# A token mixer on 272 tokens in a row instead of three blocks of 128 with empty rows, attention heads in pairs, and a decay broadcast in one pass

## The reference, cut to what matters

```python
h = concat([meta, x])                                  # (272, 1024)
z, xbc, dt_raw, q_a, kv_a, gates = split(rms_norm(h) @ w_in)
xs, bm, cm = split(silu(causal_conv4(xbc)))            # 2048, 4*128, 4*128 channels
dt = softplus(dt_raw + dt_bias); a_cs = cumsum(-exp(a_log) * dt)
y[l] = sum(s <= l) (cm[l] . bm[s]) * exp(a_cs[l] - a_cs[s]) * dt[s] * xs[s]   # per head
y_ssd = group_norm((y + d_skip * xs) * silu(z)) @ w_ssd_out
q = rms_norm(q_a) @ w_uq;  k, v = rms_norm(c_kv) @ w_ukv   # 16 heads, 64 + 32 rope; k_pe shared
y_mla = softmax(causal(q @ k.T)) @ v @ w_o
h = h + (g_ssd * y_ssd + g_mla * y_mla) @ w_out
h = h + moe(rms_norm(h))                               # 32 experts, w1 8 MB and w2 4 MB each
out = rms_norm(h)[16:]
```

## Time and profile before

| | |
|---|---|
| median of 3 runs | 1399.79 us (1399.71 to 1402.7) |
| the profiled execution: its time, its span | 1400.83 us, 1399.0 us |
| busy in the span | PE 96%, VectorE 35%, ScalarE 23%, GpSimd 5% |
| granted PE clock, mean | 0.997 |
| HBM traffic | 461.8 MB moved, 330 GB/s on average, 416 to 419 GB/s from 490 us to the last 35 us |

### The profile page before, as it was taken

One profiled execution on the slowest core, in us unless ns is written; L12 is line 12 of the kernel. 1 busy time (PEld: TensorE's weight loads), 2 busy tenths in 40 slices (PEclk: granted clock), 3 DMA queues, 4 the chain that ended last, 5 costly groups with the idle time before them and its releaser, 6 DMA issues.

```text
span 1399.0 us, 18726 instructions
## 1 busy us (share of the span) xinstructions
PE 1337.8 (96%) x7131; PEld 652.9 (47%) x7131; DVE 484.5 (35%) x1217; ACT 320.9 (23%) x630; POOL 74.5 (5%) x88
## 2 busy tenths in 40 slices
PE   8999999999999999999999999999999999999995
PEld 5867778889994333333323222223222223333331
DVE  6847779998743212111211111111111211121112
ACT  4445547765321111111111011011001011011101
POOL 1000002322303000000000000000000000000000
PEclk9999999999999999999999999999999999999999
DMA  6332131334778899999999999999999999999995
GB/s 244 129 128 114 61 121 61 122 121 181 277 299 328 353 418 418 418 416 416 418 419 418 419 417 416 418 418 418 419 417 416 417 416 417 418 419 419 417 416 229
DMA packets 77410, 461.80 MB, mean 330 GB/s; under 512 B 6848, under 2 KB 6848, under 8 KB 41136
## 3 DMA queue, kind: packets, MB, share of 16 engines
q1 hardware_dynamic: 76608, 458.64, 80.8%
q0 software_dynamic: 752, 2.49, 0.5%
HBM read 460.05 MB, written 1.05 MB: 330 GB/s over the span
## 4 chain that ended last, share of the span: by engine, by line
PE 60%; DMA 19%; SPq 16%; DVE 2%; issue 2%; ACT 1%; ACTq 0%; DVEq 0%
PE bank L1299 57%; DMA ring<-w_dram 19%; SPq L405 9%; SPq L372 6%; PE bank L1614 1%; PE bank L1620 1%; PE bank L1425 1%; DMA work<-x_dram 0%; PE bank L1407 0%; PE bank L1636 0%; DVE split L887 0%; PE bank L1482 0%; DVE work L924 0%; PE bank L1326 0%; ACT split L553 0%
## 5 line engine op out<-in xcount | busy, mean ns | idle before, releaser
L1299 PE MATMUL bank<-ring,work 128*64 128x512 f32 (+3 forms) x2264 | 548.5, 591 | 34.5 <-DMA ring<-w_dram 32.1
L1299 PE MATMUL bank<-work 128*64 128x512 f32 (+7 forms) x2168 | 445.7, 558 | 6.2 <-issue 1.9
L1299 PEld LDWEIGHTS bank<-ring,work 128*64 128x64 f32 (+1 forms) x2264 | 176.7, 142 | 355.9 <-issue 259.7
L1299 PEld LDWEIGHTS bank<-work 128*64 128x64 f32 (+4 forms) x2168 | 151.3, 144 | 261.7 <-issue 245.6
L1247 DVE COPY work<-bank 128x256 f32<-128x256 f32 x32 | 13.6, 424 | 496.4 <-PE bank L1636 496.4
L1299 PE MATMUL bank<-hn_hi,split 128*128 128x256 f32 (+1 forms) x896 | 173.3, 289 | 0.9 <-DVE split L887 0.5
L1299 PEld LDWEIGHTS bank<-hn_hi,split 128*128 128x128 f32 x896 | 142.3, 190 | 1.7 <-issue 0.9
L1299 PE MATMUL bank<-hn_lo,split 128*128 128x256 f32 (+1 forms) x448 | 127.5, 285 | 0.0
L1221 DVE TENSOR_SCALAR work<-bank 128x256 f32<-128x256 f32 x64 | 24.2, 419 | 273.9 <-PE bank L1299 273.9
L887 DVE TENSOR_TENSOR split<-ring,split 128x1024 fp32r<-128x1024 f32 x80 | 99.1, 1240 | 26.0 <-ACT split L553 25.7
L739 ACT ACTIVATE work<-bank 128x512 f32<-128x512 f32 x32 | 19.1, 597 | 331.5 <-PE bank L1299 331.5
(11 more groups left out here) (250 smaller groups left out, 948.2 us busy)
## 6 DMA issues: line engine op xcount, KB each, us to landing
ring<-w_dram SPq DMA_DIRECT2D x256, 1024.0 KB, 21.4
work<-w_dram SPq DMA_DIRECT2D x128, 1024.0 KB, 19.9
ring<-slabs_dram SPq DMA_DIRECT2D x23, 2048.0 KB, 7.4
ring<-slabs_dram SPq DMA_DIRECT2D x2, 1152.0 KB, 5.2
ring<-slabs_dram SPq DMA_DIRECT2D x1, 1536.0 KB, 11.6
ring<-slabs_dram SPq DMA_DIRECT2D x1, 1280.0 KB, 8.4
work<-x_dram SPq DMA_DIRECT2D x2, 512.0 KB, 4.8
work<-x_dram POOLq DMA_DIRECT2D x2, 512.0 KB, 17.0
```

What stands on the lines that cost most here:

```text
L1299: return pe.matmul(o, lhsT, rhs, start=start, stop=stop)
```

## The change

- **Tokens in a row.** The sequence is 272 rows in blocks of 128, 128 and 16 (`BLOCKS`). Every matrix that had 384 columns or a third block of 128 rows has 272 or 16. The block order is (0, 1, 2). The queries start at row 16, so the products over earlier tokens are cut at 112 and 240: CB, `decay` and ssdy take 256, 144 and 16 columns. Empty rows are no longer set to zero. The factors for the queries (`rsxq`) come from two small matmuls with a shifted identity.
- **Heads in pairs.** `k_pair` makes the keys of two heads in one 128-wide matmul pair; the rope rows are laid out so that the odd head lies in the other half, and a query block is 128 rows. `pv_pair` runs for two heads with alternating halves of the output. The probabilities' transposes are three of 128 columns and two of 32 rows.
- **One-pass decay broadcast.** `AT` is made four times over (one per 32 partitions), high in two quarters and low in the other two, so that one matmul with 64 rows adds both parts.
- **One convolution tap on ScalarE.** `conv_in` makes the first tap and the bias with a second activation; `conv` has three buffers.
- Inputs' order: the first block of x and the meta tokens are loaded first.

```diff
-T = NB * P
-T0 = P - NMETA
+BLOCKS = [(0, P), (P, P), (2 * P, L - 2 * P)]
+TAIL = L - 2 * P
...
-        ORDER = (1, 2, 0)
+        ORDER = (0, 1, 2)
...
-            sp.dma_start(xtok[:, 1, :], x[0:P, :]).then_inc(x_in[1], 16)
+            sp.dma_start(xtok[NMETA:P, 0, :], x[0:P - NMETA, :]).then_inc(x_in[0], 16)
+            sp.dma_start(xtok[0:NMETA, 0, :], meta).then_inc(x_in[0], 16)
             sp.dma_start(vec[:, :], vecs).then_inc(vec_in, 16)
-            sp.dma_start(xtok[:, 2, :], x[P:2 * P, :]).then_inc(x_in[2], 16)
-            sp.wait_ge(meta_zero, 1)
-            sp.dma_start(xtok[T0:P, 0, :], meta).then_inc(x_in[0], 16)
+            sp.dma_start(xtok[:, 1, :], x[P - NMETA:2 * P - NMETA, :]).then_inc(x_in[1], 16)
+            sp.dma_start(xtok[0:TAIL, 2, :], x[2 * P - NMETA:SEQ, :]).then_inc(x_in[2], 16)
...
-                a.activation(xraw[:, c % 2, 3:3 + L], ps[:, 0:L], ACT.Copy).then_inc(proj_read, 1)
+                a.activation(xraw[:, c % 2, 3:3 + L], ps[:, 0:L], ACT.Copy)
...
+                if c >= 3:
+                    a.wait_ge(conv_fin, c - 2)
+                a.activation(conv[:, c % 3, :], ps[:, 0:L], ACT.Identity, scale=v("conv_w", 4 * c + 3, 1),
+                             bias=v("conv_b", c, 1)).then_inc(proj_read, 1)
...
-                a.activation(pT[:, 0:512], bank[4][:, :], ACT.Copy).then_inc(pTa_ready, 1)
+                a.activation(pT[:, h % 2, 0:3 * P], bank[4][:, 0:3 * P], ACT.Copy).then_inc(pTa_ready, 1)
...
-                link(d.tensor_scalar(dst, src[:, 3:3 + L], v("conv_w", 4 * c + 3, 1), v("conv_b", c, 1), ALU.mult, ALU.add))
...
-                d.tensor_copy(pT[:, 512:640], bank[5][:, 0:P]).then_inc(pTb_ready, 1)
+                d.tensor_copy(pT[0:TAIL, h % 2, 3 * P:PT_COLS], bank[5][0:TAIL, 0:64]).then_inc(pTb_ready, 1)
...
-                                CBm[:, c // CHUNKS_PER_GROUP, :].unsqueeze(1).to_broadcast([P, 2, 640]),
+                                CBm[:, c // CHUNKS_PER_GROUP, :].unsqueeze(1).to_broadcast([P, 2, DECAY]),
...
-            mm(bank[2][0:HEADS_S, 0:SEQ], dAb[0], metarows[:, :], True, False)
-            mm(bank[2][0:HEADS_S, P:SEQ], dAb[2], tri[:, 0:P], False, False)
-            mm(bank[2][0:HEADS_S, 0:SEQ], dAb[1], tri[:, :], False, True)
...
+            for i in range(4):
+                o = bank[2][i * HEADS_S:(i + 1) * HEADS_S, :]
+                mm(o[:, 0:SEQ], dAb[0], tri[:, NMETA:L], True, False)
+                mm(o[:, P - NMETA:SEQ], dAb[1], tri[:, 0:P + NMETA], False, False)
+                mm(o[:, SEQ - TAIL:SEQ], dAb[2][0:TAIL, :], tri[0:TAIL, 0:TAIL], False, True)
...
-                for k in range(KKV):
-                    mm(bank[6][0:NOPE, 0:L], ukv[:, k, h * NOPE:(h + 1) * NOPE], ckvT[:, k, T0:T], k == 0, k == KKV - 1)
+                for k in range(KKV):
+                    last = mm(bank[6][:, 0:L], ukv[:, k, i * P:(i + 1) * P], ckvT[:, k, :], k == 0, k == KKV - 1)
...
-                mm(o, vh[0], pT[:, 0:SEQ], True, False)
-                mm(o[:, P:SEQ], vh[2], pT[:, 2 * SEQ:2 * SEQ + P], False, False)
-                mm(o, vh[1], pT[:, SEQ:2 * SEQ], False, True).then_inc(pv_done, 1)
...
+                for b, rows, lo, at, cols in ((0, P, 0, 0, SEQ), (1, P, P, 2 * P, P), (1, TAIL, P - 32, 3 * P, 32),
+                                              (2, TAIL, SEQ - 32, 3 * P + 32, 32)):
+                    for j in range(2):
+                        last = mm(bank[3][j * VH:(j + 1) * VH, lo:lo + cols], V[0:rows, b, (2 * i + j) * VH:(2 * i + j + 1) * VH],
+                                  pT[0:rows, j, at:at + cols], at == 0, b == 2)
...
-                    row = head_row[:, 2 * c + j:2 * c + j + 1].to_broadcast([P, P])
-                    mm(bank[2 + 2 * j][:, 0:SEQ], row, AT_hi[:, :], True, False)
-                    last = mm(bank[2 + 2 * j][:, 0:SEQ], row, AT_lo[:, :], False, True)
+                    half = slice(j * 2 * E, (j + 1) * 2 * E)
+                    last = mm(bank[2 + 2 * j][:, 0:SEQ], head_row[half, 2 * c + j:2 * c + j + 1].to_broadcast([2 * E, P]),
+                              AT_hi[half, :])
```

More of the change, by code:

```diff
@@ L130, in meta_ssd_mla_moe @@
         ident2 = sb("ident2", E + 1)
-        small = sb("small", 804)
+        small = sb("small", 808)
         idx = sb("idx", 16, U32)
@@ L246, in meta_ssd_mla_moe @@
         nrt = sm(801, 3)
+        rsxq = sm(804, 2)
         def sem(name):
@@ L598, in _ @@
             a.wait_ge(latent_trans, 1)
-            for i in range(2):
-                a.activation(kTh[NOPE:QH, i, :], bank[7][NOPE:QH, T0:T], ACT.Copy).then_inc(kpeT_ready, 1)
+            a.activation(kTh[NOPE:P, 0, :], bank[7][NOPE:P, 0:L], ACT.Copy).then_inc(kpeT_ready, 1)
+            a.activation(kTh[0:NOPE, 1, :], bank[7][0:NOPE, 0:L], ACT.Copy).then_inc(kpeT_ready, 1)
             for c in range(4, 8):
@@ L613, in _ @@
             a.wait_ge(cum_read, 1)
-            a.activation(head_row[:, :], ident[:, 0:HEADS_S], ACT.Copy)
             a.activation(AT_hi[:, :], AT[:, :], ACT.Copy).then_inc(AT_hi_ready, 1)
@@ L838, in rstd_col @@
             def rstd_col(y, src, n, eps, done):
-                tmp = nrt[:, 0:1]
+                tmp = nrt[0:y.shape[0], 0:1]
                 yi = y.bitcast(I32)
@@ L1338, in _ @@
                     pe.wait_ge(rsx_ready, 3)
-                    for c in range(NB):
-                        last = mm(bank[6][:, c * P:(c + 1) * P], rsx[:, c:c + 1].to_broadcast([P, P]), ident[:, :])
-                    last.then_inc(rsx_spread, 1)
+                    for c, (s0, m) in enumerate(BLOCKS):
+                        mm(bank[6][:, s0:s0 + m], rsx[0:m, c:c + 1].to_broadcast([m, P]), ident[0:m, 0:m])
+                    mm(bank[7][:, 0:2], shifted[:, P:2 * P], rsx[:, 0:2], True, False)
+                    mm(bank[7][:, 0:2], shifted[0:NMETA, 0:P], rsx[0:NMETA, 1:3], False, True).then_inc(rsx_spread, 1)
             wsl = take("qa").rearrange("p (k n) -> p k n", k=KD)
@@ L1445, in _ @@
             for h in range(MH):
+                if h % 2 and h + 1 < MH:
+                    k_pair((h + 1) // 2)
                 if h + 1 < MH:
-                    qk_head(h + 1)
-                feature_unit("cv", 8 + h, 8 + h, T0)
-                if h:
-                    pv_head(h - 1)
+                    q_head(h + 1)
+                feature_unit("cv", 8 + h, 8 + h, 0)
+                if h and h % 2 == 0:
+                    pv_pair(h // 2 - 1)
                 if h + 1 < MH:
@@ L1453, in _ @@
                 probs_trans(h)
[L1454 to L1455 removed]
+            feature_unit("z", 0, PZ, NMETA)
+            pv_pair(KD - 1)
             pe.wait_ge(pv_read, KD)
             for g in range(GROUPS):
[L1460 to L1465 removed]
+                ps = bank[4 + g]
+                for (t0, n), (lo, at) in zip(BLOCKS, DECAY_AT):
+                    last = mm(ps[0:n, at:at + SEQ - lo], BT[:, g, t0:t0 + n], CT[:, g, lo:SEQ])
+                last.then_inc(cb_done, 1)
             def acum_of(c):
@@ L1480, in xtr_of @@
                     pe.wait_ge(xdt_ready, c)
-                for b in range(NB):
-                    last = pe.transpose(bank[6][:, b * P:(b + 1) * P], xT[:, c, b * P:(b + 1) * P], ident[:, :])
+                for b, (t0, n) in enumerate(BLOCKS):
+                    last = pe.transpose(bank[6][0:n, b * P:(b + 1) * P], xT[:, c, t0:t0 + n], ident[:, :])
                 last.then_inc(xtr_done, 1)
```

337 lines of the change are left out of this document (174 added, 163 removed).

## The result

The changed kernel took 1381.7 us (median of 4 runs, 1380.49 to 1382.79) beside 1401.24 us for the kernel before (1399.71 to 1403.13): the ratio is 0.9863, with a 95% interval of 0.985 to 0.9876. That is 19.5 us less where 24.5 were forecast; the time lies inside the range of 1363 to 1385 and 6.7 us above the 1375 predicted. Of these 6.7 us, 1.45 lie in the kernel before, whose median of four runs is 1401.24 where three had given 1399.79. Three disturbed executions (1470.72 us of experiment 11, and 4699.71 and 6317.84 us of the kernel before, measured again beside the experiments) are left out of the ratios. The profiled execution took 1382.37 us with a span of 1380.6, 18.4 us less than the span in the earlier trace rows.

A forecast was written before the change was run, and what follows sets the result against it. The PE was taken to set the mixer and weight loads the experts, with mixer savings moving everything behind forward. Terms summed to 24.5 us less, from 1399.8 to 1375.3, said as 1375; 8-in-10 range 1363 to 1385.

The forecast's parts named there:

- the tap: Convolution's first tap moved from VectorE to ScalarE, 0.42 us per unit off VectorE; costed at nothing.
- the rival: VectorE sets stage 3's chunks, its long step's loss beside GpSimd not shrinking with columns; 1379 to 1385, chance 0.15.
- the heads: Stage 2's 16 attention heads: period 7.06 us to become 5.93 through paired keys and values.
- Keys: Stage 2 key matmuls: a pair of heads costs what one did, 1.06 us; 8.5 us less.
- Values: Stage 2 value products: two heads side by side, 1.25 us a pair with narrow matmuls at 0.13; 9.5 us less.
- narrow ones nearly free: Rival: narrow matmuls of 16 or 32 columns cost almost nothing, through alternation; 1363 to 1369 us, chance 0.20.
- CB: CB matmuls between stages 2 and 3: 4.89 us to become 3.58, four narrow ones included; 1.3 us less.
- Running sums: Row form of the sums before the queries, made four times over: 1.20 us becomes 3.52; 2.3 us more.
- Chunks: Stage 3's 16 chunks: product 1.23 to 1.03 us, 3.2 less; broadcast two passes fewer, 3.8 less; period 5.10.
- the change of tile shape costs: Rival: PE empties at 64 places with new weight rows, 0.13 us each; 1379 to 1387 chance 0.12, slower end 0.03.
- its bounds: Outer cases: narrow matmuls at 0.03 us give 1365, broadcast halves side by side 1363; narrow at 0.22 give 1385.
- Start: First microseconds: row zeroing and load order hidden beside loads, 0.5 us either way otherwise; small transposes 0.5 us less.

The follow-up runs named there:

- experiment 11: Changed kernel plus decay broadcast on 128 rows, row sums in turn, and unread matmuls in the router's, first expert's and start's waits; median 1375.5 us.
- experiments 5 and 6: Changed kernel with the narrow matmuls of value and chunk products left out, then issued twice; medians 1376.46 and 1385.64 us.
- experiment 2: Changed kernel with the four copies of the row sums alternating inside each product instead of one after the other; median 1378.82 us.
- experiment 1: Changed kernel with the decay broadcast made by matmuls on all 128 rows instead of 64; median 1379.54 us, ratio 0.9847 to the kernel before.
- Experiment 10: Changed kernel with unread matmuls in the waits at the start: 12 before the first transposes, 6 for the second block, 6 before dkv; median 1379.26 us.
- Experiment 3: Changed kernel with ten unread matmuls in the router's waits and five more in the first expert; median 1378.57 us.

## Why the prediction was right, and where its steps failed

**Right in kind:** the PE set both mixer stages, what it lost moved everything behind it, and the loads followed without a new wait. VectorE didn't take over (4.67 us a chunk by 44.10/50 x 5.30, forecast 4.72), and the tap cost the PE nothing. VectorE's long step took 1.26 us on average over the 16 chunks, 1.03 where it was shortest and 1.56 where it was longest: a loss of 0.53 us on 832 columns after one of 0.46 on 1280, so the rival was right that it doesn't shrink with the columns, and wrong in what VectorE needs in all. That the total fell inside the range is partly luck: the heads gave 2.7 us more than forecast while the start and the stretch behind the projections gave 4.0 and 2.9 less.

**Keys:** 1.02 us a pair, forecast 1.06.

**Values:** "I take the middle, 0.13, for every narrow matmul" was mis-sized: experiments 5 and 6 give 0.057 each and 0.12 for the change of shape, and the wide ones take 0.80 (1.61 less 0.81 for the scores), so a pair's values cost 0.80 + 0.23 + 0.12 = 1.15 where 1.25 was forecast. For one narrow matmul by itself 0.13 was close (0.117); what the prediction left out of the sum is that the narrow ones of two heads also run side by side, which it had as the condition of its rival "narrow ones nearly free". The estimate from the Trainium skill (TensorEngine Tiling (Array Packing), Instruction Overhead), 0.05, came near 0.057 by luck: it was worked out for a matmul by itself, and there 0.117 was measured. With transposes at 0.57 instead of 0.64 us, and scores at 0.71 instead of 0.81 in every second head, the heads gave 20.7 us, not 18.0.

**CB:** 4.07 us (192.36 to 196.43), forecast 3.58. Its four narrow matmuls, with no second head beside them, cost (4.07 - 3.06) / 4 = 0.25 each, change of shape included.

**Running sums:** 3.82 us for the row form, forecast 3.52; a cost that only the order of twelve matmuls made (experiment 2). The argument used for the values, that matmuls to different columns run side by side in turn, was not asked of this loop.

**Chunks:** the product came out, 1.05 for 1.03. The broadcast took 0.32, not 0.66 - 0.24 = 0.42: its two matmuls, on different rows, start 0.003 us apart, so they run side by side, which the prediction had only in its bounds. What failed is that a step was priced without its neighbour: weights on 64 rows made `gsum` 0.28 us longer, 13 x 0.28 = 3.6 us. It was a rival ("the change of tile shape costs", 0.13 a place), at a flat price; measured are 0.28 where 64-row weights follow 128-row ones and 0.12 where 16-row ones do. The rule of the Trainium skill (TensorEngine Tiling (Array Packing), Key Properties: a change of mode drains the engine) agrees with both, and experiment 1 shows the first by taking the change away.

**Start:** "work of the first microseconds, beside the loads ... 0.5 us either way" failed most, 3.5 us lost for 0.5 gained. By the rows: dkv starts 0.69 us later, with a wait for its slab that wasn't there; it then runs at half pace (1.79); the spread of the norm factors takes 1.48 instead of 0.67 us, 0.62 of it two matmuls for `rsxq`, which the prediction had put beside the PE though the PE makes them; 0.2 for the rest. Experiment 10 shows the second. How early the clock first rises isn't set by the change alone: in the profiled runs without unread matmuls at the start it rose between 15.25 and 17.97 us, and the first unit of B started between 38.10 and 39.77.

**The router:** no term at all. The clock there cost 1.7 us before and 5.0 after in the two profiled runs. Part of the 3.3 us is chance: over all undisturbed executions the mean clock is 0.9960 in 31 of the kernel before and 0.9948 in the 4 of the changed one, about 1.2 us by the estimate above. Experiment 3 held the clock there in its profiled run, and the other runs show that its fall isn't regular.

## What to carry to other kernels

Price a step of the PE together with its neighbours: a change in the number of rows of the weights keeps the next weights from being loaded early (0.11 to 0.28 us each time here), while matmuls to different groups of columns, put in turn, cost as one (3.82 us became 1.00). A few microseconds of PE waits can cost twice, since the PE may run at half its clock afterwards; where the waits can't be avoided, unread matmuls in them were worth about 3 us here (1381.7 to 1378.57), some of it chance. When a median moves by 2 to 4 us, read the clock and the last waits before crediting the edit.

## What the hardware showed unexpectedly

Four matmuls with weights of 32 columns ran side by side at the price of one. A narrow matmul (16 or 32 columns on 16 rows, float32) cost 0.057 us where two ran side by side, 0.117 by itself. The granted clock of a stretch at the start can read 1.00 while matmuls come at half pace, since the record begins with the clock's first rise. And the wait ahead of the final scatter, 1.90 us before and 2.17 in the changed kernel, ranged from 1.90 to 3.01 us over the runs, and with more instructions in the program it split in two, 5.06 us in all.
